# Half of the summed down blocks by seven products, two of the four weight sums by adding transfers

## The chip, the cores and the metric

The kernel runs on one core of one Trainium2 chip. The metric is the device time of one execution in microseconds (us), lower is better; the time of the kernel before is the median of three runs. Engines are named as in the profile: PE is TensorE, ACT is ScalarE, DVE is VectorE, POOL is GpSimd, SP is SyncE, whose queue issues nearly all loads.

## The reference, cut to what matters

```python
x = x + einsum(merged, w_out)                        # three kinds of mixers, 16 heads
x = x + cross_attention(rms_norm(x, g_cross), mem_n, w_cq, w_ckv, w_co)
u = jnp.einsum('bsd,df->bsf', rms_norm(x, g_mlp[l]), w_up[l])
x = x + jnp.einsum('bsf,fd->bsd', jnp.square(jax.nn.relu(u)), w_down[l])
return rms_norm(x, g_final)
```

There is one layer, 256 tokens and a width of 2048; the hidden width of the last block (the MLP) is 8192. All is float32. The MLP's two products take more than half of the time, and the change lies in the second of them, the down product hidden (256 x 8192) by w_down (8192 x 2048), but for one small move ahead of it.

## The kernel before, in words

**Splitting.** Each weight is used as a high part plus a low part. A megabyte of weights is loaded by SP into one of four `staged` slots. ACT writes the high part of a half (128 x 1024) to `w_high`, DVE subtracts it from the staged half and writes `w_low`, and PE multiplies: high by high, low weight by high activation, high weight by low activation. `w_high` and `w_low` hold four halves each; half h uses place h % 4, so ACT may split it only when PE is done with half h - 4. The counts are semaphores: `landed` (a slot has arrived), `high_ready`, `low_ready`, `half_done`. SP waits on `low_ready`, since a slot is free when its last half was split.

**The MLP.** The hidden width is done in four quarters. In a quarter, 16 up jobs (two halves each) make 16 tiles of 128 hidden channels, `part_b`; each goes from PE through ACT and DVE (`up`). Then comes the quarter's share of the down product. Quarter 3 does it plainly, into `x`. Quarters 0 to 2 (`SUMMED_QUARTERS`) do it with tokens as rows: outputs are 128 tokens by 512 columns, one matmul 128 x 512 at a time.

**A group.** In such a quarter there are two groups g of 1024 output columns. A group has four units of 512 hidden channels (four tiles). Three units are done directly by `r_half`: four halves of 12 matmuls each, into the PSUM tensors `extra[0..3]`. One unit, unit 0, is taken as a 2 x 2 block product (two halves of the tokens, of the channels and of the columns) and done by seven products in place of eight (Winograd's form): `s_half`, seven halves of 6 matmuls each. That needs sums of activations (`sums_of_tokens`, into `part_s`) and four sums of weight blocks (`sum_of_weights`, DVE, in place in the staged slots). Halves 0 to 2 multiply plain blocks, halves 3 to 6 are unit 1, halves 7 to 10 multiply the summed blocks (`H_SUMS`), halves 12 to 19 are units 2 and 3 (`H_B`, `H_C`). In all a group has 7 x 6 + 12 x 12 = 186 matmuls. At its end the results go by twelve DVE adds of 128 x 512 (`step`) into `y`, which is `values`. In quarter 3 PE turns `y` back by transposes between the up jobs, and DVE adds it to `x`.

**What sets the order.** It is written out by hand: each engine runs its own list in order, with semaphore waits. In the down part SP loads a unit as two transfers of 1 MB (`load_unit`, of w_down, 2 KB pieces), each as soon as its slot's last half is split. DVE's list is `down_group`: weight sums, low splits and steps, with the splits of the next group (`next_group`) or quarter at its end. PE's list is `down_group` too.

**Ahead of the MLP.** `norm_sum` is one small matmul on PE that sums the squares of the tokens, which POOL accumulates. It stands right after the first job that uses the new x, both before the cross attention (N_X1) and before the MLP (N_X2). POOL also clears `y` (line 411), and DVE waits for that before its first split of the MLP.

## Time and profile before

| | us |
|---|---|
| median of 3 runs | 1203.58 (1203.50 to 1203.62) |
| the profiled execution's own time | 1203.42 |
| its span in the trace | 1201.6 |
| PE busy | 1182.1, 98% of the span |
| DVE busy | 853.1, 71% |
| ACT busy | 628.7, 52% |
| POOL busy | 177.8, 15% |
| DMA, mean rate | 187 GB/s |

The granted TensorE clock was 0.998 of full. The span is 1.8 us less than the time of the same execution. Busy time of an engine in the page is time in which at least one of its instructions runs; successive matmuls overlap, so the mean duration of a matmul in the groups (389 ns) is more than the distance between two of them. That distance is read from the timeline. In the trace the three summed quarters' down parts lie near 571 to 656, 747 to 833 and 922 to 1008 us.

### The profile page before, as it was taken

The numbers are of one execution on the slowest core, as the hardware profiler recorded it, in microseconds if no ns is written. First come the engines' busy times: TensorE is split into PE (matmuls) and PEld (weight loads), VectorE is DVE, ScalarE is ACT, GpSimd is POOL, SyncE is SP. The second block draws the span as 40 slices with busy tenths as digits, with TensorE's granted clock in tenths as the row PEclk, the third lists the DMA queues.
The fourth block names the chain that finished last, engine by engine and source line by source line (L and its number), as shares of the span: only waits on it lengthen the run. The fifth ranks groups of instructions, "written<-read, shape, count | busy, mean of one in ns | idle before, by whom it ended". The sixth has DMA issues, their size and how long they took to land.

```text
span 1201.6 us, 19272 instructions
## 1 busy us (share of the span) xinstructions
PE 1182.1 (98%) x6776; PEld 1035.6 (86%) x6776; DVE 853.1 (71%) x1149; ACT 628.7 (52%) x927; POOL 177.8 (15%) x177
## 2 busy tenths in 40 slices
PE   9999999999999999999999999999999999999996
PEld 7888899999989889888788888788888888888885
DVE  5758766786668867676887666877767787666554
ACT  6445455555645657555544555544655454555442
POOL 2907400030322404200000000000000000000341
PEclk9999999999999999999999999999999999999999
DMA  9674553443644543456456454547543746555531
GB/s 357 252 260 173 196 175 140 162 154 140 246 162 165 181 159 142 151 198 209 166 176 253 175 181 168 210 149 271 175 176 139 264 157 220 191 182 187 198 140 70
DMA packets 51455, 224.43 MB, mean 187 GB/s; under 512 B 3792, under 2 KB 4176, under 8 KB 31696
## 3 DMA queue, kind: packets, MB, share of 16 engines
q1 hardware_dynamic: 50688, 220.22, 50.8%
q10 hardware_dynamic: 720, 3.59, 0.8%
q8 instruction: 30, 0.49, 0.2%
q14 instruction: 17, 0.14, 0.0%
HBM read 221.69 MB, written 2.10 MB: 186 GB/s over the span
## 4 chain that ended last, share of the span: by engine, by line
PE 93%; DVE 3%; ACT 1%; issue 1%; POOL 1%; DMA 1%; SPq 0%; DVEq 0%; ACTq 0%; POOLq 0%
PE bank L1301 16%; PE bank L1298 16%; PE bank L1299 15%; PE extra L1557 6%; PE extra L1559 5%; PE extra L1558 5%; PE bank L1303 4%; PE bank L1305 4%; PE bank L1304 4%; PE bank L1344 3%; PE bank L1346 3%; PE bank L1345 3%; DVE w_low L813 1%; PE bank L1570 1%; PE bank L1571 1%
## 5 line engine op out<-in xcount | busy, mean ns | idle before, releaser
L813 DVE TENSOR_TENSOR w_low<-staged,w_high 128x1024 fp32r<-128x1024 f32 x311 | 390.0, 1269 | 145.5 <-ACT w_high L433 134.9
L433 ACT ACTIVATE w_high<-staged 128x1024 fp32r<-128x1024 f32 x304 | 314.6, 1053 | 189.8 <-PE bank L1301 81.2
L1299 PEld LDWEIGHTS bank<-part_a,w_low 128*128 128x128 f32 x1408 | 264.6, 188 | 61.4
L1298 PE MATMUL bank<-part_a,w_high 128*128 128x512 f32 x704 | 281.0, 399 | 0.0
L1301 PE MATMUL bank<-part_a,w_high 128*128 128x512 f32 x704 | 278.5, 396 | 0.0
L1299 PE MATMUL bank<-part_a,w_low 128*128 128x256 f32 x1408 | 276.8, 278 | 0.0
L719 ACT ACTIVATE w_high<-staged 128x1024 fp32r<-128x1024 f32 x114 | 118.9, 1058 | 108.9 <-PE extra L1559 92.0
L1133 DVE TENSOR_TENSOR w_low<-staged,w_high 128x1024 fp32r<-128x1024 f32 x114 | 137.4, 1221 | 33.8 <-ACT w_high L719 32.6
L361 POOL TENSOR_TENSOR squares<-x 128x256 f32<-128x256 f32 (+1 forms) x31 | 37.3, 1204 | 685.2 <-DVE x L1257 661.3
L1298 PEld LDWEIGHTS bank<-part_a,w_high 128*128 128x128 f32 x704 | 133.7, 190 | 0.6 <-DVE w_low L813 0.3
L1301 PEld LDWEIGHTS bank<-part_a,w_high 128*128 128x128 f32 x704 | 132.0, 187 | 0.0
L1557 PE MATMUL extra<-w_high,part_b 128*128 128x512 f32 x288 | 112.7, 391 | 3.2 <-DVE w_low L1133 2.2
L1559 PE MATMUL extra<-w_high,part_b 128*128 128x512 f32 x288 | 112.1, 389 | 0.0
L1558 PE MATMUL extra<-w_low,part_b 128*128 128x512 f32 x288 | 112.1, 389 | 0.0
L1303 PE MATMUL bank<-part_a,w_high 128*128 128x256 f32 x384 | 110.2, 287 | 0.1
L1305 PE MATMUL bank<-part_a,w_low 128*128 128x256 f32 x384 | 108.7, 283 | 0.0
L1304 PE MATMUL bank<-part_a,w_high 128*128 128x256 f32 x384 | 108.6, 283 | 0.0
L1098 DVE TENSOR_TENSOR part_b<-hidden,part_b 128x256 f32 (+1 forms) x64 | 27.2, 426 | 71.6 <-ACT part_b L701 71.6
L1303 PEld LDWEIGHTS bank<-part_a,w_high 128*128 128x128 f32 x384 | 73.7, 192 | 0.5 <-POOL part_a L375 0.4
L1304 PEld LDWEIGHTS bank<-part_a,w_high 128*128 128x128 f32 x384 | 73.6, 192 | 0.1
L1305 PEld LDWEIGHTS bank<-part_a,w_low 128*128 128x128 f32 x384 | 73.6, 192 | 0.0
L1557 PEld LDWEIGHTS extra<-w_high,part_b 128*128 128x128 f32 x288 | 54.0, 188 | 16.7 <-issue 5.1
(201 smaller groups left out, 1775.1 us busy)
## 6 DMA issues: line engine op xcount, KB each, us to landing
staged<-in_wup SPq DMA_DIRECT2D x64, 1024.0 KB, 4.8
staged<-in_wdown SPq DMA_DIRECT2D x64, 1024.0 KB, 5.0
staged<-in_wqk SPq DMA_DIRECT2D x32, 1024.0 KB, 4.8
staged<-in_wv SPq DMA_DIRECT2D x12, 1024.0 KB, 5.4
staged<-in_wbc SPq DMA_DIRECT2D x8, 1024.0 KB, 4.8
staged<-in_wmk SPq DMA_DIRECT2D x4, 1024.0 KB, 4.7
staged<-in_woa SPq DMA_DIRECT2D x4, 1024.0 KB, 4.8
staged<-in_wcq SPq DMA_DIRECT2D x4, 1024.0 KB, 4.8
```

Of the source, the lines that this page charges most:

```text
L433: nc.scalar.activation(w_high[:, job % 2, cols], staged[:, job % 4, cols], ACT.Copy).then_inc(high_ready, 1)
L813: tt(w_low[:, job % 2, cols], staged[:, job % 4, cols], f32(w_high[:, job % 2, cols]), ALU.subtract).then_inc(low_ready, 1)
L1133: tt(half_4d(w_low, h), src, f32(half_4d(w_high, h)), ALU.subtract).then_inc(low_ready, made)
L1298: mm(out[:, :], high, both, start=first, stop=False)
L1299: last = mm(out[:, 0:T], low, part[:, slot(kt), 0, :], start=False, stop=False)
L1301: last = mm(out[:, :], high, both, start=False, stop=last_tile)
L1303: mm(out[:, 0:T], high, part[:, slot(kt), 0, :], start=first, stop=False)
L1304: mm(out[:, 0:T], high, part[:, slot(kt), 1, :], start=False, stop=False)
L1305: last = mm(out[:, 0:T], low, part[:, slot(kt), 0, :], start=False, stop=last_tile)
L1557: mm(out[:, :], part_b[:, kt, 0, tokens], high, start=opens, stop=False)
L1558: mm(out[:, :], part_b[:, kt, 0, tokens], low, start=False, stop=False)
L1559: last = mm(out[:, :], part_b[:, kt, 1, tokens], high, start=False, stop=ends)
```

## The change

**Units 0 and 2 by seven products.** A group is now two pairs, each of one unit by seven products and one unit done directly: four pairs in a quarter (`PAIRS`), each with halves 0 to 2 plain blocks, 3 and 4 the direct unit's first part, 5 to 8 the summed blocks (`H_T`), 10 and 11 the direct unit's rest. A pair has 7 x 6 + 4 x 12 = 90 matmuls, a group 180. Sums of activations are made for both units.

**Products summed in PSUM.** The seven products of pair 0 stay in their PSUM places and those of pair 1 are added there. DVE then adds all eight places to `y` in four adds of 128 x 1024 a group, and `y` now holds the raw products in eight blocks a group; a second array `y_right` is added for it. The recombination (`combine`, seven DVE operations a group) is done once, during quarter 3. The transposes there follow in its second half.

**Two weight sums by transfers.** The sign form of the sums is changed so that all are additions. Two of the four are made by POOL's queue: `weights_onto` issues transfers from DRAM with an adding write onto the staged block, two of 128 x 4 x 128 float32 (256 KB, in 512 B pieces) for each sum. The first sum waits for the landing of the second slot; the second one waits also for the split of the first block. ACT waits on `right_sum` and `upper_sum`, and DVE on `upper_sum` ahead of its own two sums.

**Slots.** The seven-product unit always uses slots 0 and 1, the direct one slots 2 and 3.

**Smaller moves.** `norm_sum` for N_X1 and N_X2 stands in the middle of the first half of the second job, no longer behind the first job. DVE's wait for the clearing of `y` stands ahead of the down part. At the end of the up jobs, the low split of half 3 (`r_tile`) stands ahead of the last `up` on ACT and DVE. `rope` shares its place with later tensors, and three loops on DVE and ACT are unrolled.

```diff
-GROUP_HALVES = 20
-GROUP_STEPS = 12
+PAIRS = 4
+PAIR_HALVES = 12
+GROUP_STEPS = 4
+H_B11, H_B21, H_B22, H_R, H_T, H_R_END = 0, 1, 2, 3, 5, 10
+SLOT_S, SLOT_R = 0, 2
...
+            def load_down(q):
+                for k in range(PAIRS):
+                    load_unit(q, k, k % 2 * 2, SLOT_S, (-2, -2) if k else (-6, -4))
+                    load_unit(q, k, k % 2 * 2 + 1, SLOT_R, (H_T - PAIR_HALVES, 0) if k else (-2, 0))
...
+            def weights_onto(q, k, to, n, row, signal):
+                unit = k % 2 * 2
+                src = wdown_in[bass.ds(q * 16 + (k // 2 * 8 + 4 * n), 4), :,
+                               512 * unit:512 * (unit + 1)].rearrange("o p (a b c) -> p b a o c", a=2, b=2)
+                for pair in range(2):
+                    pool.dma_start(to[:, pair, :, :], src[:, row, pair, :, :], accum_op=ALU.add).then_inc(signal, 16)
+
+            with pool.Fori(0, SUMMED_QUARTERS) as q:
+                for k in range(PAIRS):
+                    pool.wait_ge(landed[SLOT_S + 1], q * 128 + 16 * (JOB_MLP // 4 + 4 + k + 1))
+                    weights_onto(q, k, by_pair(SLOT_S + 1, 0), 1, 1, right_sum)
+                    pool.wait_ge(low_ready, down_half(q, k) + 1)
+                    weights_onto(q, k, by_pair(SLOT_S, 0), 1, 0, upper_sum)
...
+                    if n < 2:
+                        act.wait_ge((upper_sum, right_sum)[n], q * 128 + 32 * (k + 1))
+                    else:
+                        act.wait_ge(weight_made, q * 8 + (2 * k + n - 1))
+                    down_high(q, k, H_T + n, by_pair(SLOT_S + col, row), 2 if n == 3 else 1)
...
+            def down_pair(q, k, ahead):
+                last = k % 2
+                r_tile(q, k, 1)
+                sum_of_weights(q, k, 2)
+                s_sum(q, k, 0)
+                sum_of_weights(q, k, 3)
+                for n in range(1, 4):
+                    s_sum(q, k, n)
+                r_tile(q, k, 2)
+                if last:
+                    step(q, k, 0)
+                r_tile(q, k, 3)
+                if last:
+                    step(q, k, 1)
                 ahead(0)
+                if last:
+                    step(q, k, 2)
                 ahead(1)
...
                 ahead(2)
+                if last:
+                    step(q, k, 3)
                 ahead(3)
...
+                if opens:
+                    pe.wait_ge(y_step, steps)
+                pe.wait_ge(s_low, q * 4 + (unit + 2))
+                s_half(q, k, H_B22, extra[2], sum_of(unit, 3), opens)
...
-                if s == 0:
-                    norm_sum(N_X1, extra[3])
```

In `load_unit` the numbers in brackets are counted from the pair's own first half: -2 is met when the last summed block (half 8, which counts twice) of the pair before is split.

POOL, between the clearing of `y` and the loop over the last norm. Before, nothing stands there:

```order
L411 MEMSET values 128x4096 [waits cross_o]
L354 MEMSET acc 128x256 [waits sum_ready]
L413 UNCONDITIONAL_BRANCH [waits acc_clear]
```

Now, the last of the four pairs in the loop over the quarters (each pair has these rows):

```order
L432 ISA [waits landed1]
L432 DMA staged<-in_wdown 128x4x128
L432 ISA
L432 DMA staged<-in_wdown 128x4x128
L438 REGISTER_ALU
L432 ISA [waits low_ready]
L432 DMA staged<-in_wdown 128x4x128
L432 ISA
L432 DMA staged<-in_wdown 128x4x128
```

Four issues a pair have come to POOL's queue, 48 in all. `landed1` is the semaphore of the second slot.

DVE, from the last tile of the up jobs into the first group of a quarter. Before:

```order
521 L1091 TENSOR_TENSOR spare<-spare,bank3 128x256 [waits up_moved]
522 L1094 SCALAR_TENSOR_TENSOR spare<-spare,factor 128x256 [waits up_added]
523 L1098 TENSOR_TENSOR part_b<-hidden,part_b 128x256 [waits hid_high]
524 L1148 TENSOR_TENSOR staged<-staged 128x2x4x128
525 L1132 REGISTER_ALU
526 L1133 TENSOR_TENSOR w_low<-staged,w_high 128x1024 [waits high_ready]
527 L1148 TENSOR_TENSOR staged<-staged 128x2x4x128
528 L1132 REGISTER_ALU
529 L1133 TENSOR_TENSOR w_low<-staged,w_high 128x1024 [waits high_ready]
530 L1148 TENSOR_TENSOR staged<-staged 128x2x4x128 [waits weight_made]
```

Now, at the same place:

```order
547 L1157 TENSOR_TENSOR w_low<-staged,w_high 128x1024 [waits high_ready]
548 L1114 REGISTER_ALU
549 L1115 TENSOR_TENSOR spare<-spare,banks 128x256 [waits up_moved]
550 L1118 SCALAR_TENSOR_TENSOR spare<-spare,factor 128x256 [waits up_added]
551 L1122 TENSOR_TENSOR part_b<-hidden,part_b 128x256 [waits hid_high]
552 L1156 REGISTER_ALU [waits y_clear]
553 L1157 TENSOR_TENSOR w_low<-staged,w_high 128x1024 [waits high_ready]
554 L1167 ISA
555 L1171 TENSOR_TENSOR staged<-staged 128x2x4x128 [waits upper_sum]
556 L1156 REGISTER_ALU
557 L1157 TENSOR_TENSOR w_low<-staged,w_high 128x1024 [waits high_ready]
```

The split of half 3 (row 526 before, 547 now) has moved ahead of the last tile's three operations, and the first weight sum that DVE makes waits for POOL's transfers; the splits of the summed blocks are queued behind it.

## Rows read from the trace of the kernel before

**Rows 1.** The page: busy time of the engines, and the chain that ended last.
```profile
PE 1182.1 (98%) x6776; PEld 1035.6 (86%) x6776; DVE 853.1 (71%) x1149; ACT 628.7 (52%) x927; POOL 177.8 (15%) x177
...
PE 93%; DVE 3%; ACT 1%; issue 1%; POOL 1%; DMA 1%; SPq 0%; DVEq 0%; ACTq 0%; POOLq 0%
```

**Rows 2.** Busy time by stretch: an up part, a down part.
```profile
core 0: us, PE busy (x) PEld busy (x) DVE busy (x) ACT busy (x) POOL busy (x), PEclk, DMA share, GB/s
660.00:747.00 87.00, 87.00 (x501) 75.90 (x501) 58.74 (x87) 49.12 (x78) 0.00 (x0) 1.00 0.51 181
747.00:834.00 87.00, 85.91 (x381) 70.55 (x380) 70.29 (x73) 42.43 (x44) 0.00 (x0) 1.00 0.56 202
```

**Rows 3.** Timeline of PE: a down part's start, group 1's start, next quarter.
```profile
747.36 0.39 PE L1570 MATMUL bank<-w_high,part_b 128*128 128x512 f32 x1
...
751.22 0.39 PE L1572 MATMUL extra<-w_high,part_s 128*128 128x512 f32 x1
752.70 0.49 PE L1557 MATMUL extra<-w_high,part_b 128*128 128x512 f32 x1 [1.09 <-DVE w_low L1133]
...
790.96 0.39 PE L1570 MATMUL bank<-w_high,part_b 128*128 128x512 f32 x1
...
833.24 0.39 PE L1298 MATMUL bank<-part_a,w_high 128*128 128x512 f32 x1
```

**Rows 4.** Timeline of PE, ACT and DVE: one half's end, and the next split.
```profile
766.20 0.39 PE L1572 MATMUL bank<-w_high,part_s 128*128 128x512 f32 x1
...
766.62 1.06 ACT L719 ACTIVATE w_high<-staged 128x1024 fp32r<-128x1024 f32 x1 [1.60 <-PE bank L1572]
...
767.72 2.59 DVE L1133 TENSOR_TENSOR w_low<-staged,w_high 128x1024 fp32r<-128x1024 f32 x2 [1.36 <-ACT w_high L719]
```

**Rows 5.** Timeline of DVE at 750 us: sums and splits back to back.
```profile
750.21 1.22 DVE L1148 TENSOR_TENSOR staged<-staged 128x1024 f32<-128x1024 f32 x1
751.35 1.22 DVE L1133 TENSOR_TENSOR w_low<-staged,w_high 128x1024 fp32r<-128x1024 f32 x1
752.48 1.22 DVE L1148 TENSOR_TENSOR staged<-staged 128x1024 f32<-128x1024 f32 x1
```

**Rows 6.** w_down's loads, 744 to 792 us: issues on SP, and time to landing.
```profile
766.52 0.93 SPq L317 DMA_DIRECT2D staged<-in_wdown  x2
770.48 0.37 SPq L317 DMA_DIRECT2D staged<-in_wdown  x1
...
DMA to landing us min/median/max: 5.0/5.1/7.8
```

**Rows 7.** The same stretch by windows of 2 us (columns as in rows 2).
```profile
770.00:772.00 2.00, 2.00 (x11) 1.63 (x10) 1.97 (x4) 1.36 (x2) 0.00 (x0) 1.00 1.05 403
772.00:774.00 2.00, 2.00 (x11) 1.65 (x10) 1.97 (x3) 1.06 (x1) 0.00 (x0) 1.00 1.08 382
```

**Rows 8.** DMA issues by size: median us from issue to landing.
```profile
out<-values SPq DMA_DIRECT2D x3, 512.0 KB, 2.8
...
out<-values SPq DMA_DIRECT2D x1, 256.0 KB, 2.1
```

**Rows 9.** Timeline of PE at the two norm sums.
```profile
407.64 0.40 PE L1301 MATMUL bank<-part_a,w_high 128*128 128x512 f32 x1
408.91 0.70 PE L1353 MATMUL extra<-acc,square 128*128 128x256 f32 x2 [0.88 <-POOL acc L370]
...
486.41 0.40 PE L1301 MATMUL bank<-part_a,w_high 128*128 128x512 f32 x1
487.94 0.70 PE L1353 MATMUL extra<-acc,square 128*128 128x256 f32 x2 [1.13 <-POOL acc L370]
```

**Rows 10.** Timeline of DVE, then PE, behind the second norm sum.
```profile
491.77 1.23 DVE L813 TENSOR_TENSOR w_low<-staged,w_high 128x1024 fp32r<-128x1024 f32 x1 [5.28 <-POOL values L411]
...
496.62 0.40 PE L1301 MATMUL bank<-part_a,w_high 128*128 128x512 f32 x1
497.03 0.50 PE L1298 MATMUL bank<-part_a,w_high 128*128 128x512 f32 x1
```

**Rows 11.** Groups of instructions: a step of before on DVE.
```profile
L1176 DVE TENSOR_TENSOR values<-values,extra 128x512 f32<-128x512 f32 x24 | 16.5, 686 | 3.3 <-PE extra L1559 2.9
```

More of the change, by code:

```diff
@@ L307, in _, with load_up @@
             stream(wco_in, JOB_CO, CROSS)
-            def load_up(q):
-                with sp.Fori(0, QUARTER // 4) as i:
+            def load_up(q, first):
+                if first:
+                    for s in range(4):
+                        load(wup_in[q * 16 + s, :, :], mlp(q), JOB_MLP + s)
+                else:
+                    for s, free in enumerate((-2, -2, H_T - PAIR_HALVES, 0)):
+                        sp.wait_ge(low_ready, mlp(q)(2) + (H_MLP + free))
+                        sp.dma_start(staged[:, s, :], wup_in[q * 16 + s, :, :]).then_inc(landed[s], 16)
+                with sp.Fori(1, QUARTER // 4) as i:
@@ L1306, in half_job, with job_of @@
                 return last
-            def job_of(off, job, n_out, part, ready=None, wide=True, slot=lambda kt: kt):
+            def job_of(off, job, n_out, part, ready=None, wide=True, slot=lambda kt: kt, between=None):
                 pe.wait_ge(taken, off(1) + (n_out + 1))
@@ L1317, in job_of @@
                     half_job(off, job, half, bank[job % 4], part, 8 * half, wide=wide,
-                             slot=slot, waits=waits).then_inc(half_done, 1)
+                             slot=slot, waits=waits, between=None if half else between).then_inc(half_done, 1)
             def short_jobs(job, n_out, part, at, waits={}):
@@ L1516, in _ @@
                     job_of(none, JOB_CQ + s, OUT_CQ + s, part_a,
[L1517 removed]
+                           x1_low if s == 0 else None, slot=slot_x1, between=N_X1 if s == 1 else None)
                 else:
```

447 lines of the change are left out of this document (210 added, 237 removed).

## The prediction

> **What bounds the kernel now.** I read the page first: PE is busy for 98% of the span and is 93% of the chain that ended last [rows 1]. Then the stretches: in an up part PE never rests, in a down part it rests 1.1 us, and DVE, the next busiest, works 70.3 of 87 us there [rows 2]. So a matmul less is worth its full distance as long as DVE, ACT and the loads keep up, and the down part has the least room for that. The distance between two matmuls is what counts, not the 389 ns of one: group 1 of quarter 1 runs from 790.96 to 833.24 us, 42.28 us for 186 matmuls, 0.2273 us each [rows 3].
>
> **Part 1, fewer matmuls.** 6 fewer in each of 6 groups: 36 x 0.2273 = 8.2 us less on PE.
>
> **Part 2, half 3 split earlier.** At the start of a down part PE has issued its last matmul of half 2 at 751.22 and could go on at 751.45, but starts half 3 at 752.70 [rows 3]. It waits for a DVE split queued behind the last tile's operations. These change places, so 1.25 us goes in each of three quarters, 3.8 us.
>
> **Part 3, the norm sums.** PE could go on at 407.87 and 486.64 but waits for POOL until 408.91 and 487.94, 1.04 and 1.30 us [rows 9]. In the middle of the next half-job POOL is done. Behind the second sum there is no slack: PE waits a little again at 497.03 for a DVE split (it could have gone on at 496.85), and DVE had itself started at 491.77 only, when POOL's clearing of `y` was over [rows 10]. The norm sum itself comes no earlier than now, but that wait for the clearing goes from there. I keep 1.1 of the 1.30: 2.1 us in both (bounds 1.2 and 2.3).
>
> **Part 4, DVE and ACT.** A step of 128 x 512 takes 686 ns [rows 11], twelve in a group; now four adds of 1024 columns take some 1.2 us each, as a split does [rows 5]. DVE's list for a group was 19 splits, 4 sums and 12 steps, 23 x 1.135 + 12 x 0.70 = 34.5 us (1.135 us is the distance of two operations back to back [rows 5]). Now it is 22 splits, 4 sums and 4 steps, 30 x 1.135 = 34.1 of 40.9 us. In quarter 3 the recombination adds 14 operations, some 11 us, over eight up jobs of 5.4 us in which DVE is busy two thirds of the time [rows 2]; I cost it at nothing, with DVE's rest as cover (without it, up to 11 us). The second unit's sums of activations lie there too, in each quarter. The longer clearing of `y` is needed only at the first down part.
>
> If nothing else were late, the sum would be 8.2 + 3.8 + 2.1 = 14.1 us less.
>
> **Part 5, where the loads now stand.** This decides. I follow one pair on PE from its start: halves 0 to 2 end at 4.09, halves 3 and 4 at 9.55, the summed halves 5 to 8 at 15.0, the pair at 20.46. Between a half's end on PE (766.43) and the next split there are 0.2 us to ACT, 1.1 to DVE's start and 1.2 for DVE [rows 4, 5], 2.5 in all. Half 8 may be split when half 4 is done, so its split is over at 9.55 + 2.5 = 12.1. That frees slots 0 and 1, and only then SP issues the next pair's two loads and the one for slot 2 behind them. A load lands 5.1 us after its issue, the second of two issued together after 7.8 [rows 6], a further one 2.7 later (1.05 MB at the 390 GB/s of [rows 7]). So slot 0 lands at 17.2, slot 1 at 19.9, slot 2 at 22.6. Half 3 of the next pair is then ready at 22.6 + 1.1 + 1.2 + 0.1 = 25.0 and due at 20.46 + 4.09 = 24.55: half a microsecond late with no adding transfer in the way. And behind an odd pair DVE has nine operations queued from 13.6 on (splits 10, 11, 0, 1, 2 and the four steps), until 23.8; PE waits for the last step ahead of half 2, due at 23.2.
>
> **Part 6, the adding transfers.** They start when slot 1 has landed. DVE's first sum waits for them, with the splits of halves 5 to 8 queued behind it: sum, split, sum, split, split, split, 6 x 1.135 + 0.1 = 6.9 us. The last of these is what frees the slots for the next pair. So there is a loop: split of half 8, loads (7.8), transfers (X), DVE (6.9). Its length is c = 14.7 + X a pair, against 20.46 on PE. X is the time from slot 1's landing to the landing of all four adding transfers (256 KB each). A quarter's down part has three such loops, 12.1 us ahead of them and 6.9 behind (half 8 and halves 10, 11 on PE): 19.0 + 3c, against 85.88 now (747.36 to 833.24 [rows 3]). Over three quarters, with part 3: 9c - 200.7 - 2.1, which is 9X - 70.5. It breaks even at X = 7.8. Ahead of pair 0 the loads come during the up jobs, and its transfers are hidden. The two ACT waits are off the path, as ACT's splits run ahead of DVE's.
>
> No transfer of POOL's queue and no adding one is in this trace, so X is bounded. From below: four issues 0.47 us apart (SP's: 0.93 for two [rows 6]) and a plain 256 KB transfer, 2.1 us [rows 8], 3.5 us. From above: four times the moving time for each, behind SP's loads, 16.1 us. A plain 256 KB costs 0.7 us of moving (2.8 less 2.1 for 256 KB more) and 1.4 around it [rows 8]. An add reads the block in DRAM and the staged block, so I take 1.4 us each, 5.6 for four. SP's two loads for slots 2 and 3 stand ahead of them on the same engines, 5.4 us of which 2.4 have passed when slot 1's landing is seen (5.1 less 2.7): 3.0. The end costs 1.4 and POOL's first issue 0.5. X = 3.0 + 5.6 + 1.4 + 0.5 = 10.5 us, c = 25.2, and the change is 9 x 10.5 - 70.5 = +24 us. The value is nearer to the lower bound since its row is a transfer of this size; the upper one is a guess at how much a piece of 512 B and an add can cost.
>
> On the same price the Trainium skill has a rule: in "DMA: Bandwidth & Descriptors", section "Anatomy of one DMA — SWDGE (gpsimd) path", a transfer issued by GpSimd takes about 2.0 us plus its bytes at 436 GB/s, an estimate of 2.6 us here. With four of them overlapping at the issue distance above, X would be 4.1 us and the loop would not bind, which is the first rival. Against it, "Collectives: The Full Stack", section "Why ReduceScatter is half of AllGather", says that an adding transfer is slower because it needs two source reads. No run here shows either yet.
>
> **The rivals.**
>
> (a) The transfers fit, X under 7.8. Then the late slot 2 and the steps of part 5 stay: 0.5 to 1.1 us for each of nine pairs and 0.6 to 0.9 for three odd pairs, 6.3 to 12.6 us, off 14.1. That gives 2 to 8 us less, and I take 5: 1198 us. For it: the plain 256 KB transfer of 2.1 us. Against it: SP's loads fill the engines (a DMA share of 1.05 and 1.08 [rows 7]) just when the transfers start.
>
> (b) All of the gain comes, 14.1 us: 1189.3 us. That needs loads some 1 us quicker than the landing times of rows 6.
>
> (c) The transfers are far slower than their plain price, X over 16. The mechanism is the same loop, at the wait of DVE's first sum in each of nine pairs; it passes 1280 us at X = 16.3, and X = 25 gives 9 x 25 - 70.5 = +154, 1358 us. Then pair 0's transfers show too. For it: pieces of 512 B, where w_down's loads have 2 KB.
>
> **How the numbers follow.** The profiled execution took 1203.42 us, 0.16 below the median of the runs, so the sum can be set against either. Forecast: 1203.4 + 24 = 1227.5 us. Chances: X between 8 and 16, slower by 2 to 77 us, 0.62; near break-even 0.04; (a) 0.15; (b) 0.06; (c) 0.13. A measurement of this kernel can tell about 0.2%, 2.4 us, from no change. Part of (a) lies within that: faster 0.18, same 0.07, slower 0.75. The range goes from 1197 to 1280: it leaves out (b), the quick end of (a), and (c). The forecast's own range is 1206 to 1280.
>
> **What would show it.** In the profile of the changed kernel: 1080 matmuls of 128 x 512 in the summed quarters, distance unchanged; no wait at half 3 of the first pair of a quarter; PE waiting at half 5, the first summed block, in pairs 1 to 3 for a DVE split, DVE's sum in turn for a transfer, together some 4 to 5 us a pair; pairs 25 us apart, slot loads issued right behind half 8's split. Wrong if the transfers land within 7.8 us of slot 1 (then half 3 and half 2 have the waits), if the longest wait stands at another half, or if the up part of quarter 3 becomes longer by more than 1 us (part 4).

## The result, and the profile after

The changed kernel took 1251.53 us (median of 4 runs, 1250.67 to 1252.63), the kernel before, run beside it, 1203.54 (1203.20 to 1203.62). The ratio is 1.0398, 95% interval 1.0383 to 1.0413: 48.0 us slower. The forecast was slower, 1227.5 us, with a range of 1197 to 1280. So the direction and the mechanism held, and half of the size was missing.

The page of the changed kernel, busy time and the chain that ended last, to be read against [rows 1]:

```profile
PE 1196.0 (96%) x6740; PEld 1037.2 (83%) x6740; DVE 869.1 (70%) x1155; ACT 644.4 (52%) x945; POOL 244.0 (20%) x226
...
PE 72%; DMA 12%; issue 6%; DVE 5%; ACT 3%; POOL 1%; SPq 0%; POOLq 0%; DVEq 0%; ACTq 0%
```

The 36 matmuls are gone (6776 before, 6740 now), and yet PE is busy for longer, because part of its work now runs at a lower clock (below). In the chain PE fell from 93% to 72%, and DMA rose from 1% to 12%. Two groups of the page name it, first an instruction group, then the DMA issues with KB each and median us to landing:

```profile
L432 POOL DMA_DIRECT2D staged<-in_wdown x48 | 62.6, 1879 | 478.9 <-DMA staged<-in_wdown 455.7
...
staged<-in_wdown SPq DMA_DIRECT2D x64, 1024.0 KB, 5.6
...
staged<-in_wdown POOLq DMA_DIRECT2D x48, 256.0 KB, 6.9
```

PE's waits of the changed kernel (engine, line and releaser; us in total, times, longest):

```profile
PE banks L1597 <- DVE w_low L1157: 30.2, 12, 4.2
PE extras L1584 <- DVE w_low L1157: 4.3, 5, 1.1
PE extras L1597 <- DVE values L1186: 1.7, 3, 0.7
```

L1597 multiplies the blocks of the seven products, plain and summed, and L1584 the direct unit. The three down parts show the whole loss (columns as in [rows 2]):

```profile
570.31:673.52 103.21, 89.51 (x361) 69.60 (x359) 66.83 (x61) 45.08 (x47) 15.59 (x12) 0.95 0.70 187
762.81:865.30 102.49, 89.95 (x362) 70.93 (x360) 66.76 (x61) 44.91 (x47) 15.63 (x12) 0.93 0.69 186
954.58:1055.63 101.05, 88.92 (x361) 69.47 (x360) 67.50 (x61) 45.59 (x47) 15.95 (x13) 0.95 0.68 186
```

They are 306.75 us together, where before they were 257.6 (85.8 and twice 85.9; the second is 747.36 to 833.24 in [rows 3]): 49.2 us more. The first down part starts 2.1 us earlier than before, and the stretch from the end of the last down part to the end of the span is as long as it was (193.4 us). DVE is busy for 67 us of these 102, so the amount of its work is no bound, as the sum of part 4 said. PE's idle time is 38.4 us of the 306.8; its 360 matmuls a quarter, 81.8 us at 0.2273 us each, keep it busy for 89.5 in the mean. Most of that excess goes with the lower granted clock (0.93 to 0.95): e10 below, at 1.00, has 83.5.

The loop that the forecast rested on stands in the timelines. First DVE's first sum in each pair of a quarter (some of the expectations call a pair a super-unit), with what its idle time ended on (start us, us, engine line op out<-in xcount):

```profile
576.65 1.22 DVE L1171 TENSOR_TENSOR staged<-staged 128x1024 f32<-128x1024 f32 x1
...
603.50 1.23 DVE L1171 TENSOR_TENSOR staged<-staged 128x1024 f32<-128x1024 f32 x1 [5.96 <-DMA staged<-in_wdown]
...
630.11 1.22 DVE L1171 TENSOR_TENSOR staged<-staged 128x1024 f32<-128x1024 f32 x1 [5.33 <-DMA staged<-in_wdown]
...
657.54 1.23 DVE L1171 TENSOR_TENSOR staged<-staged 128x1024 f32<-128x1024 f32 x1 [6.45 <-DMA staged<-in_wdown]
```

The pairs follow each other at 26.85, 26.61 and 27.43 us, against the 20.46 that PE needs. One turn of the loop, from the chain of waits between 610 and 637 us:

```profile
610.46 0.37 SPq L328
...
610.87 7.41 DMA staged<-in_wdown
...
618.94 0.06 POOL staged L432
...
621.17 8.91 DMA staged<-in_wdown
...
635.82 1.23 DVE w_low L1157
637.06 0.37 SPq L328
```

SP issues when half 8 is split, the second of the two loads has landed 7.8 us later, from 618.3 POOL issues and the transfers move until 630.1, and DVE's sums and splits take 6.95 us until SP is released again. That is 7.8 + 11.8 + 7.0 = 26.6.

### The profile page after: what moved, and what is told of

Its sections match the earlier page's. It is cut to its first block, busy times and chain, and to the rows that moved or that the text cites. A ratio compares the mean times of both kernels' runs of the same rounds, so it can differ in the third digit from the quotient of the medians.

```text
span 1249.0 us, 19107 instructions
## 1 busy us (share of the span) xinstructions
PE 1196.0 (96%) x6740; PEld 1037.2 (83%) x6740; DVE 869.1 (70%) x1155; ACT 644.4 (52%) x945; POOL 244.0 (20%) x226
## 3 DMA queue, kind: packets, MB, share of 16 engines
q0 software_dynamic: 25344, 12.59, 8.1%
## 4 chain that ended last, share of the span: by engine, by line
PE 72%; DMA 12%; issue 6%; DVE 5%; ACT 3%; POOL 1%; SPq 0%; POOLq 0%; DVEq 0%; ACTq 0%
PE banks L1326 15%; PE banks L1329 15%; PE banks L1327 15%; DMA staged<-in_wdown 10%; PE banks L1331 5%; PE banks L1333 5%; PE banks L1332 5%; PE banks L1372 3%; PE banks L1374 3%; PE banks L1373 3%; DVE w_low L1157 2%; ACT w_high L748 1%; POOL staged L432 1%; DMA staged<-in_wup 1%; DVE staged L1171 1%
## 5 line engine op out<-in xcount | busy, mean ns | idle before, releaser
L837 DVE TENSOR_TENSOR w_low<-staged,w_high 128x1024 fp32r<-128x1024 f32 x311 | 390.1, 1269 | 135.5 <-ACT w_high L461 130.6
L1327 PEld LDWEIGHTS banks<-part_a,w_low 128*128 128x128 f32 x1408 | 264.6, 188 | 61.7
L1326 PE MATMUL banks<-part_a,w_high 128*128 128x512 f32 x704 | 280.5, 398 | 1.4 <-DVE w_low L837 1.4
L1329 PE MATMUL banks<-part_a,w_high 128*128 128x512 f32 x704 | 278.5, 396 | 0.0
L1327 PE MATMUL banks<-part_a,w_low 128*128 128x256 f32 x1408 | 276.8, 278 | 0.0
L1157 DVE TENSOR_TENSOR w_low<-staged,w_high 128x1024 fp32r<-128x1024 f32 x132 | 157.4, 1221 | 50.3 <-ACT w_high L748 49.8
L432 POOL DMA_DIRECT2D staged<-in_wdown x48 | 62.6, 1879 | 478.9 <-DMA staged<-in_wdown 455.7
L1326 PEld LDWEIGHTS banks<-part_a,w_high 128*128 128x128 f32 x704 | 133.7, 190 | 2.7 <-DVE w_low L837 2.5
L1329 PEld LDWEIGHTS banks<-part_a,w_high 128*128 128x128 f32 x704 | 131.9, 187 | 0.0
L1331 PE MATMUL banks<-part_a,w_high 128*128 128x256 f32 x384 | 110.1, 287 | 0.1
L1333 PE MATMUL banks<-part_a,w_low 128*128 128x256 f32 x384 | 108.7, 283 | 0.0
L1332 PE MATMUL banks<-part_a,w_high 128*128 128x256 f32 x384 | 108.6, 283 | 0.0
L1584 PE MATMUL extras<-w_high,part_b 128*128 128x512 f32 x192 | 75.5, 393 | 4.3 <-DVE w_low L1157 4.3
L1585 PE MATMUL extras<-w_low,part_b 128*128 128x512 f32 x192 | 74.8, 390 | 0.0
L1586 PE MATMUL extras<-w_high,part_b 128*128 128x512 f32 x192 | 74.8, 389 | 0.0
L1331 PEld LDWEIGHTS banks<-part_a,w_high 128*128 128x128 f32 x384 | 73.7, 192 | 0.5 <-POOL part_a L387 0.4
L1332 PEld LDWEIGHTS banks<-part_a,w_high 128*128 128x128 f32 x384 | 73.6, 192 | 0.1
L1333 PEld LDWEIGHTS banks<-part_a,w_low 128*128 128x128 f32 x384 | 73.6, 192 | 0.0
L725 ACT ACTIVATE hidden<-spare 128x256 f32<-128x256 f32 x64 | 26.8, 418 | 85.6 <-DVE spare L1118 85.6
```

The source lines that it names most:

```text
L432: pool.dma_start(to[:, pair, :, :], src[:, row, pair, :, :], accum_op=ALU.add).then_inc(signal, 16)
L837: tt(w_low[:, job % 2, cols], staged[:, job % 4, cols], f32(w_high[:, job % 2, cols]), ALU.subtract).then_inc(low_ready, 1)
L1157: tt(half_4d(w_low, h), src, f32(half_4d(w_high, h)), ALU.subtract).then_inc(low_ready, made)
L1326: mm(out[:, :], high, both, start=first, stop=False)
L1327: last = mm(out[:, 0:T], low, part[:, slot(kt), 0, :], start=False, stop=False)
L1329: last = mm(out[:, :], high, both, start=False, stop=last_tile)
```

## The experiments

All are compared with the kernel before, run on the same chip beside them. Times are medians.

| run | us | ratio to before, interval |
|---|---|---|
| changed kernel | 1251.53 | 1.0398 (1.0383 to 1.0413) |
| e1_plain | 1227.41 | 1.0197 (1.0180 to 1.0214) |
| e2_slot2_first | 1255.97 | 1.0430 (1.0413 to 1.0448) |
| e3_dve_sums | 1227.81 | 1.0192 (1.0175 to 1.0209) |
| e4_small_moves | 1201.86 | 0.9985 (0.9976 to 0.9995) |
| e5_upper_first | 1231.15 | 1.0231 (1.0214 to 1.0248) |
| e6_right_by_dve | 1222.06 | 1.0154 (1.0137 to 1.0170) |
| e7_rotated | 1239.11 | 1.0294 (1.0277 to 1.0311) |
| e8_rotated_upper_first | 1225.14 | 1.0183 (1.0166 to 1.0200) |
| e9_before_four_first | 1197.02 | 0.9946 (0.9932 to 0.9959) |
| e10_rotated_right_by_dve | 1201.56 | 0.9984 (0.9974 to 0.9994) |
| e11_rotated_dve_sums | 1203.64 | 1.0001 (0.9992 to 1.0011) |

### e1: the same transfers without the adding

```diff
-                    pool.dma_start(to[:, pair, :, :], src[:, row, pair, :, :], accum_op=ALU.add).then_inc(signal, 16)
+                    pool.dma_start(to[:, pair, :, :], src[:, row, pair, :, :]).then_inc(signal, 16)
```

> The changed kernel with the adding write left out of POOL's 48 transfers: they overwrite the staged block (so two of the four weight sums are not made), all waits and sizes as they are. Theory: the loop of a pair (DVE's split of half 8, slot loads, transfers X, DVE) sets the time, and X = 11.8 us is 0.6 to POOL's start, 5.2 of four issues of 1.30 us, and 6.0 to the last landing. If the add itself (two reads) makes the 6.0 long, a plain write ends X near 0.6 + 5.2 + 2.1 = 7.9 us: nine loops by 3.9 us, 35 us less, 1216 us. Rival 1, queueing behind SP's two loads makes it long: X falls by the second read alone, at most 0.7 us each for the last two, 1.4: 1239 us. Rival 2, the small pieces (512 B) and not the add: no change, 1251 us.

Measured: 1227.41 us, 24 us less than the changed kernel, midway between the 1216 of the theory and the 1239 of the first rival. POOL's issues of one pair, from the timeline of POOL, first in the changed kernel and then in e1:

```profile
591.89 5.18 POOL L432 DMA_DIRECT2D staged<-in_wdown  x4 [23.50 <-DMA staged<-in_wdown]
```

```profile
591.72 2.96 POOL L432 DMA_DIRECT2D staged<-in_wdown  x4 [24.61 <-DMA staged<-in_wdown]
```

And DVE's first sums in e1:

```profile
601.11 1.22 DVE L1171 TENSOR_TENSOR staged<-staged 128x1024 f32<-128x1024 f32 x1 [3.75 <-DMA staged<-in_wdown]
...
624.78 1.22 DVE L1171 TENSOR_TENSOR staged<-staged 128x1024 f32<-128x1024 f32 x1 [2.46 <-DMA staged<-in_wdown]
```

Windows of e1 behind the loads (columns as in [rows 2]):

```profile
596.00:598.00 2.00, 1.73 (x8) 1.42 (x9) 1.35 (x2) 0.00 (x0) 0.00 (x0) 1.00 1.04 303
598.00:600.00 2.00, 2.00 (x10) 1.69 (x9) 0.00 (x0) 0.00 (x0) 0.00 (x0) 1.00 0.60 168
```

An issue takes 0.74 us in place of 1.30, and this loop is 23.7 us in place of 26.6; in the mean of all nine it is 24.3 in place of 26.8, so X is 9.6 us where the adding form needs 12.1. The plain transfers move at 303 GB/s from 596 to 598 us and are nearly through by 600, the adding ones at 166 to 192 until 602 (the windows are shown further below). So the adding form costs 2.5 us for four transfers, nine times, and half of the whole loss. What in it costs that, the adding itself or its smaller packets, is not shown: the plain transfers went in 80 packets each, the adding ones in 528. Nor does e1 show what makes the other half; e3, below, loses as much without any transfer of POOL's, though with two more sums a pair on DVE.

### e2 and e5: other orders of the same transfers

e2 has SP load slot 2 of the next pair as soon as half 4 is split, ahead of slots 0 and 1:

```diff
                 for k in range(PAIRS):
+                    if k:
+                        load_unit(q, k, k % 2 * 2 + 1, SLOT_R, (H_T - PAIR_HALVES, 0), (0,))
                     load_unit(q, k, k % 2 * 2, SLOT_S, (-2, -2) if k else (-6, -4))
-                    load_unit(q, k, k % 2 * 2 + 1, SLOT_R, (H_T - PAIR_HALVES, 0) if k else (-2, 0))
+                    load_unit(q, k, k % 2 * 2 + 1, SLOT_R, (H_T - PAIR_HALVES, 0) if k else (-2, 0),
+                              (1,) if k else (0, 1))
```

> The changed kernel with SP's load of slot 2 for pairs 1 to 3 issued ahead of the loads of slots 0 and 1 (its slot is free much earlier, after the split of half 4 of the pair before), so that 1 MB less stands ahead of the adding transfers on the DMA engines; SP's loop over the quarters is unrolled for it. Theory that the transfers queue behind SP's loads: X falls by up to 2.7 us, nine loops, 24 us less, 1227 us, and PE's wait at half 3 of pairs 1 and 3 goes. Rival, X is POOL's issues and the transfer itself: X stays at 11.8, the time at 1250 us, only the wait moves from half 3 to half 5.

Measured: 1255.97 us, 4.4 slower than the changed kernel, where I had expected 1227 and the rival said 1250. Windows of e2 after POOL's issues at 592.06 (columns as in [rows 2]), then DVE's first sum:

```profile
594.00:596.00 2.00, 2.00 (x11) 1.69 (x10) 2.00 (x2) 0.51 (x1) 2.00 (x3) 1.00 1.25 161
596.00:598.00 2.00, 2.00 (x11) 1.65 (x10) 0.14 (x1) 0.00 (x0) 1.24 (x1) 1.00 1.31 156
...
600.00:602.00 2.00, 1.09 (x5) 0.56 (x3) 0.00 (x0) 0.00 (x0) 0.00 (x0) 1.00 1.09 305
```

```profile
606.22 1.23 DVE L1174 TENSOR_TENSOR staged<-staged 128x1024 f32<-128x1024 f32 x1 [10.08 <-DMA staged<-in_wdown]
```

With fewer loads ahead of them the adding transfers move early (161 and 156 GB/s from 594), but then the load for slot 2 of the next pair, issued at 596.16, comes among them, and the sum can only start at 606.22, 14.2 us after POOL's first issue. The megabyte was moved from ahead of the transfers into them, and nothing was won.

e5 issues the upper sum's transfers ahead of the right one's:

```diff
-                    pool.wait_ge(landed[SLOT_S + 1], q * 128 + 16 * (JOB_MLP // 4 + 4 + k + 1))
-                    weights_onto(q, k, by_pair(SLOT_S + 1, 0), 1, 1, right_sum)
                     pool.wait_ge(low_ready, down_half(q, k) + 1)
                     weights_onto(q, k, by_pair(SLOT_S, 0), 1, 0, upper_sum)
+                    pool.wait_ge(landed[SLOT_S + 1], q * 128 + 16 * (JOB_MLP // 4 + 4 + k + 1))
+                    weights_onto(q, k, by_pair(SLOT_S + 1, 0), 1, 1, right_sum)
```

> The changed kernel with POOL's two sums in the other order: the upper one, which DVE's first sum and half 5 need, is issued first, the right one, needed by half 6, behind it. Waits and sizes as they are. Theory: the transfers run after SP's loads at 1.4 us each, the upper sum then lands 2.8 us earlier; the right one, landing where the upper one did, holds half 6 by some 0.5 us; each of nine loops is 2.3 us shorter: 21 us less, 1231 us. Rival, half 8's split needs all four transfers in any order: nothing changes, 1251 us.

Measured: 1231.15 us, as expected. DVE's sum waits for the upper sum alone, so only two of the four transfers stand in the loop ahead of it: it starts at 600.64 in place of 603.50, and what comes late of the other two is a wait of 0.5 us for the right sum's half behind it. The order of two pairs of issues on POOL is worth 20 us here.

### e3 and e6: sums by DVE in place of transfers

e3 has all four sums made by DVE and no transfer by POOL; e6 only the right one.

```diff
             def down_pair(q, k, ahead):
...
+                sum_of_weights(q, k, 0)
                 r_tile(q, k, 1)
-                sum_of_weights(q, k, 2)
+                sum_of_weights(q, k, 1)
                 s_sum(q, k, 0)
-                sum_of_weights(q, k, 3)
-                for n in range(1, 4):
-                    s_sum(q, k, n)
+                sum_of_weights(q, k, 2)
+                s_sum(q, k, 1)
+                sum_of_weights(q, k, 3)
+                s_sum(q, k, 2)
+                s_sum(q, k, 3)
```

> The changed kernel with all four weight sums of a pair made by DVE, none by transfers; POOL issues nothing. Theory: the loop loses X and gets two DVE operations. From slot 1's landing at 7.8 us DVE has the split of half 2, then, from slot 2's landing at 10.5, ten operations of 1.135 us to the end of half 8's split: c = 10.5 + 1.1 + 11.4 = 23 us, one more with steps between: 9 x 23.5 - 202.7 = +9 against before, 1205 to 1222 us. Rival, the loads or the lower granted clock make the down part long and not X: less than 10 us are gained, 1240 us or more.

```diff
             def down_pair(q, k, ahead):
                 last = k % 2
+                tt(by_pair(SLOT_S + 1, 0), by_pair(SLOT_S + 1, 0), by_pair(SLOT_S + 1, 1),
+                   ALU.add).then_inc(right_sum, 1)
                 r_tile(q, k, 1)
...
-                    weights_onto(q, k, by_pair(SLOT_S + 1, 0), 1, 1, right_sum)
```

> The changed kernel with the right sum made by DVE (one operation ahead of half 4's split, while it would wait anyway) and the upper one alone by two transfers. Theory: X loses two transfers of 1.4 us each and two issues, about 3.4 us; the DVE operation is hidden in DVE's wait for the upper sum: nine loops, 31 us less, 1221 us. Rival, it is DVE that has no room (four sums on DVE gave 1227.8 us): the operation costs its 1.1 us in each of 12 pairs: 1233 us.

Measured: e3 1227.81 us, above the 1205 to 1222 that I had expected, e6 1222.06, as expected. At e3 I took PE's many waits of 0.5 to 1.1 us for a VectorE at its limit. Its timeline says otherwise:

```profile
591.35 2.36 DVE L1141 TENSOR_TENSOR w_low<-staged,w_high 128x1024 fp32r<-128x1024 f32 x2 [3.65 <-ACT w_high L735]
...
638.57 2.36 DVE L1141 TENSOR_TENSOR w_low<-staged,w_high 128x1024 fp32r<-128x1024 f32 x2 [3.70 <-ACT w_high L735]
```

DVE stands still for 3.7 us, for ACT, and ACT for a load; the two rows are two pairs apart, and in the pair between, which has the four steps on DVE, it is 1.8 us. The loop of the slots' reuse (split of half 8, then the load of both slots of the seven-product unit, then the splits) is there without any transfer of POOL's; it is only shorter (23.7 us from the first sum at 597.91 to the next pair's at 621.63). That gave e7.

### e7 and e8: rotated slots

The seven-product unit has two loads, called its first and second S block here. The first S block of the next pair goes into the slot that half 4's split frees, no longer into one that the sums hold until half 8's:

```diff
-SLOT_S, SLOT_R = 0, 2
+SLOTS_OF = ((0, 1, 2, 3), (2, 0, 1, 3), (1, 2, 0, 3), (0, 1, 2, 3))
...
                 for k in range(PAIRS):
+                    s_slots, r_slots = SLOTS_OF[k][:2], SLOTS_OF[k][2:]
+                    if k:
+                        load_unit(q, k, k % 2 * 2, s_slots, (H_T - PAIR_HALVES, -2), (0,))
+                        load_unit(q, k, k % 2 * 2, s_slots, (H_T - PAIR_HALVES, -2), (1,))
+                    else:
+                        load_unit(q, k, 0, s_slots, (-6, -4))
+                    load_unit(q, k, k % 2 * 2 + 1, r_slots, (-2, 0))
```

> The changed kernel with slots that rotate from pair to pair, (0,1,2,3), (2,0,1,3), (1,2,0,3), (0,1,2,3) for the summed unit's two and the direct unit's two: the next pair's first block goes to the slot that is free after half 4's split, and only the second one and the direct unit's first wait for half 8's split. POOL's order as in the change, SP's loop over the quarters unrolled. Theory: the loop that sets the time is slot release, load, transfers, DVE; with the first block loaded some 7 us earlier the loads ahead of the transfers are fewer, and slot 1's landing comes 2.7 us earlier. The upper sum would land near 29.4 us in the pair's clock and is due at 27.5: 1.9 us late in nine pairs: 1194 + 17 = 1211 us (1200 to 1225). Rival, the engines' total work (four loads and four transfers in the same place) sets the landing, as in the run with slot 2's load moved: 1245 us or more.

e8 is e7 with the order of e5 on POOL.

> The same rotated slots with the upper sum's transfers first. They wait for the split of the first block, over at 17.7 us of the pair before, and land near 25 where 27.5 is due, so the waits at half 5 go; the right sum is at most 0.5 us late for half 6. Theory: all that is left of the change's cost is the step behind odd pairs: 14.1 us less than before but for some 4 to 6 us, 1194 to 1199 us, faster than the kernel before. Rival, POOL's own issues (1.30 us each, and 3.9 us of standing still once a quarter) hold pairs whatever the slots: 1205 to 1215 us.

Measured: 1239.11 and 1225.14 us, both far above what I had expected (1211, and 1194 to 1199); the first stays under its rival's 1245, the second is above its rival's 1205 to 1215 too. The windows of e7 behind POOL's first issue at 590.19:

```profile
592.00:594.00 2.00, 2.00 (x11) 1.65 (x10) 0.52 (x1) 1.61 (x2) 2.00 (x3) 1.00 1.05 387
594.00:596.00 2.00, 2.00 (x11) 1.65 (x10) 1.84 (x2) 0.51 (x1) 1.37 (x2) 1.00 1.30 188
596.00:598.00 2.00, 2.00 (x10) 1.66 (x9) 0.00 (x0) 0.00 (x0) 0.00 (x0) 1.00 1.46 185
...
600.00:602.00 2.00, 1.57 (x7) 0.95 (x6) 0.00 (x0) 0.00 (x0) 0.00 (x0) 1.00 1.12 341
```

and DVE's next sum there:

```profile
605.31 1.23 DVE L1176 TENSOR_TENSOR staged<-staged 128x1024 f32<-128x1024 f32 x1 [9.46 <-DMA staged<-in_wdown]
```

Two things show. The loads still come first (387 GB/s until 594), the adding transfers then fill the engines for six microseconds at 185 to 200 GB/s, and a further load comes before the last of them has ended: 15.1 us from POOL's first issue to the sum. And the loop is not gone. The second S block still waits for half 8's split, and the right sum is added onto just that block, so every pair still has a split, a load and an adding transfer in a row, with one load in it in place of two. Its second turn is 605.31 to 629.40, 24.1 us. In e8 the upper sum is out of that row, but the right one is not, and ACT waits for it (4.3 us ahead of its split at 603.19).

### e10 and e11: the rotation with the right sum, or all sums, by DVE

e10 is e7 with the edit of e6, e11 is e7 with the edit of e3.

> The changed kernel with the loads into rotated slots of e7, and the second weight sum by VectorE instead of POOL's adding transfers, as in e6: what is left to the adding transfers is 512 KB a super-unit, two issues of POOL. Theory (DMA order): e7 and e8 lost most of what the rotation should give because POOL's adding transfers moved only behind SP's loads that were already in the queues (first pair of e7: share 1.05 at 387 GB/s till 594, then 1.3 to 1.46 at 185 to 200 GB/s for 6 us, so 15.1 us from POOL's first issue at 590.19 to VectorE's sum at 605.31). With half as many transfers that queue costs 2.9 us less and PE's waits of 4 to 6 us at the first pair fall to 1 to 3; VectorE, with 4.9 us more of sums a quarter, keeps its waits of 0.5 to 1.1 us at some eight places a quarter, as in e6. Down parts 89 to 92 us, time 1211 to 1219, say 1215. Rival 1 (VectorE is the bound of the hybrid): the same as e6, 1220 to 1224, waits of PE all for w_low with VectorE without idle time ahead of them. Rival 2: both were independent losses and go together, down parts of 86 to 87 us and 1200 to 1205, which would bring the family level with the kernel before.

> The changed kernel with all four weight sums by VectorE, as in e3, and the rotated slots of e7: POOL adds nothing, no transfer reads a block a second time. Theory: in e3 the bound was not VectorE's work but the loop of a slot's reuse: VectorE stood 3.65 to 3.70 us before half splits at 591.35 and 638.57, for ACT, which stood 3.8 us for the load of a block whose slot the sums had held. Its work in two super-units of e3 is 21.7 and 17.7 us (597.91 to 645.4 without its idle time), 19.7 in the mean against the 20.5 us that PE needs for one. With the load early, that wait is gone, and what is left are PE's waits of 0.5 to 1 us where VectorE runs through its 21.7 us stretch. Down parts of 84 to 89 us instead of 94.3, 95.8 and 93.6: 1227.8 - 3 x 8 = 1203, range 1196 to 1210. So the adding transfers of e10 (1201.6) would be worth about nothing, 2.3 us of VectorE a super-unit against waits for DRAM. Rival 1 (VectorE is the bound): the waits stay as in e3 at every fourth half and the time is 1215 to 1228. Rival 2 (transfers were the whole rest): below 1196, level with the kernel of e9.

Measured: e10 1201.56 us, in the second rival's 1200 to 1205 and 13 us below what I had expected; e11 1203.64, as expected. PE's waits in the down parts, of e10, then of e11:

```profile
PE banks L1602 <- DVE w_low L1160: 3.9, 6, 1.6
PE extras L1602 <- DVE values L1189: 1.8, 3, 0.6
```

```profile
PE banks L1587 <- DVE w_low L1146: 2.9, 6, 0.6
...
PE extras L1587 <- DVE values L1173: 1.3, 3, 0.5
```

The 30.2 us of waits of the changed kernel for the low parts of these blocks are down to 3 or 4. So it was the place of the loads and transfers that cost the time, and not the seven products for two units: with the right sum on DVE, no transfer has to wait for the late block any more. The down parts are 86.3, 87.9 and 83.7 us in e10 and 86.8, 87.1 and 85.8 in e11, against 85.8 and twice 85.9 before. All that 2.7 us less of matmuls a quarter brings, 8.2 us in all, is spent again where PE waits for DVE: the matmuls that start later than 0.2273 us behind the one before, nearly all of them at the start of a half that a DVE result released, add up to 12.2 us in e10's three down parts and 13.4 in e11's, against 4.2 before. DVE is 29 us (e10) and 42 us (e11) busier than before (882.1 and 894.8 against 853.1 in [rows 1], the recombination of quarter 3 among it).

Two adding transfers a pair, in place of one sum by DVE, gain 2.1 us here (e10 against e11, whose intervals of the ratio just touch) and 5.8 us with the old slots (e6 against e3). And e10 and e11 have the small moves in them. The kernel before with an order of the same kind, e9 below, takes 1197.02 us, 4.5 less than e10: no run of this study shows the new arithmetic ahead of the old one.

### e4 and e9: the small moves, in the kernel before

e4 is the kernel before with the three smaller moves: `norm_sum` in the middle of the next job, DVE's wait for the clearing later, and half 3's split ahead of the last `up`.

```diff
                 for n in range(count):
+                    if between is not None and n == count // 2:
+                        norm_sum(between, extra[3])
...
-                if s == 0:
-                    norm_sum(N_X1, extra[3])
...
+                    if s == 3:
+                        r_tile(q, 0, 3, SLOT_RA[0], 0)
                     up(q, 3, s)
...
                         sum_of_weights(q, 0, 0)
-                        r_tile(q, 0, 3, SLOT_RA[0], 0)
...
+                dve.wait_ge(y_clear, 1)
                 down_group(q, 0, next_group(q))
```

> The kernel before with the change's small moves alone: the two norm sums in the middle of the next half-job, DVE's wait for the clearing of y ahead of the down part, and the split of half 3 ahead of the last tile's operations on ACT and DVE. One unit of four by seven products, all as before. Theory (parts 2 and 3 of the prediction): 3.8 + 2.1 = 5.9 us less, 1197.7 us (0.995 of before). Rival, the wait at half 3 comes back at the first weight sum, which is now behind: 2.1 us less, 1201.4 us.

Measured: 1201.86 us, the rival's value. Timeline of DVE, then of PE, at the start of the first down part:

```profile
574.89 2.35 DVE L1148 TENSOR_TENSOR staged<-staged 128x1024 f32<-128x1024 f32 x2
577.16 1.22 DVE L1133 TENSOR_TENSOR w_low<-staged,w_high 128x1024 fp32r<-128x1024 f32 x1
...
578.43 0.50 PE L1558 MATMUL extra<-w_high,part_b 128*128 128x512 f32 x1 [1.15 <-DVE w_low L1133]
```

The wait at half 3 is gone and stands at half 4, as long as before: two of DVE's differences of weights are ahead of its split. In the changed kernel no sum of DVE's stands there, so there the move gained what it should.

e9 puts half 4's split ahead of the first difference too:

```diff
                     else:
+                        r_tile(q, 0, 3, SLOT_RA[0], 1)
                         sum_of_weights(q, 0, 0)
...
-                sum_of_weights(q, g, 1)
-                r_tile(q, g, 3, ra, 1)
-                sum_of_weights(q, g, 2)
-                r_tile(q, g, 3, ra, 2)
-                sum_of_weights(q, g, 3)
-                r_tile(q, g, 3, ra, 3)
+                if g:
...
+                else:
+                    r_tile(q, g, 3, ra, 2)
+                    sum_of_weights(q, g, 1)
+                    r_tile(q, g, 3, ra, 3)
+                    sum_of_weights(q, g, 2)
+                    sum_of_weights(q, g, 3)
```

> The kernel before with the small moves of e4 (norm sums behind the first half of the next job, the wait for the cleared outputs later, half 3's split ahead of the last up chunk's) and one more: for the first super-unit of a quarter the split of half 4 stands ahead of VectorE's first difference of weight blocks, those of halves 5 and 6 each behind one difference. Theory: what swallowed the gain of half 3's move in e4 was a wait of PE for half 4's split (1.24 us on PE at 578.43, 753.62 and 928.83), which came late because two differences (2.36 us) stood ahead of it on VectorE. Half 4's high part is ready by 575.4, its split then ends near 576.6, and PE reaches the half at 577.1; the half of difference later still leaves the sums' splits (due from 585.3) more than 1 us. So the wait goes in all three pairs: 1201.9 - 3 x 1.25 = 1198.1, first down at 570.3 as before the change of order, the down part 84.7 to 84.9 long instead of 86.0. Rival: the wait moves on once more, to half 5 or 6 or to the first weight sum, and the time stays at 1201 to 1202. A second rival: only the first quarter gains, since later ones start with VectorE behind, 1200.5.

Measured: 1197.02 us, as expected (1198.1), 6.5 us below the kernel before (ratio 0.9946, 0.9932 to 0.9959) and the fastest of this study. DVE's timeline:

```profile
575.86 1.23 DVE L1133 TENSOR_TENSOR w_low<-staged,w_high 128x1024 fp32r<-128x1024 f32 x1 [0.52 <-ACT w_high L719]
577.00 1.22 DVE L1148 TENSOR_TENSOR staged<-staged 128x1024 f32<-128x1024 f32 x1
```

PE no longer waits anywhere in the three down parts, which last 84.5 us each. What beat the kernel before is an order of a few instructions, with none of the new arithmetic.

## Why the prediction was right, and where it fell short

**Part 1 held.** PE runs 36 matmuls fewer, 0.227 us apart where its clock is full (for instance from 668.64 to 672.50, 17 steps of 0.2271). The saving is real, and covered by waits.

**Part 2 held in the changed kernel,** where no wait stands at half 3 of a quarter's first pair. That it would be worth 3.8 us by itself did not: e4 shows the same wait at the next half, until e9 moved that too.

**Part 3 held.** The first down part starts at 570.31 us, where it was 572.39: 2.08 us, predicted 2.1.

**Part 4 held.** Quarter 3 and what follows take 193.4 us as before, with the 14 recombinations in it, and the steps cost no more than said.

**Part 5 held in its order and was short in its head.** Slot 2 is late as said: the five waits at L1584 (up to 1.1 us) are its waits, and the three for `values` (up to 0.7 us) are those for the last step ahead of half 2. But half 8's split of the first pair ends 13.2 us after the pair's start and not at 12.1. The sum let it hang on PE's half 4 alone. In the trace DVE starts its list at 575.50, late because of the last tile's operations, and then runs without a rest until 583.5, so the length of DVE's list decides:

```profile
575.50 1.23 DVE L1157 TENSOR_TENSOR w_low<-staged,w_high 128x1024 fp32r<-128x1024 f32 x1 [0.53 <-ACT w_high L748]
...
580.05 3.49 DVE L1157 TENSOR_TENSOR w_low<-staged,w_high 128x1024 fp32r<-128x1024 f32 x3
```

The first sum stands 6.34 us into the down part, forecast 5.2: 1.1 us in each quarter, 3.4 in all.

**Part 6: the mechanism was right, X was mis-sized.** The load (7.8 us) and DVE's share (6.9, measured 6.95) are as forecast. X was taken as 10.5, and over the nine loops it comes to 12.1 (26.8 - 14.7; the nine take 241.1 us). This is the term that failed, and the windows between POOL's first issue at 591.9 and the sum at 603.5 say which part of it:

```profile
592.00:594.00 2.00, 2.00 (x11) 1.58 (x10) 1.33 (x2) 0.44 (x1) 2.00 (x3) 1.00 1.05 386
594.00:596.00 2.00, 1.50 (x7) 0.91 (x5) 0.82 (x1) 1.92 (x2) 2.00 (x3) 1.00 1.05 381
596.00:598.00 2.00, 1.54 (x7) 1.28 (x8) 1.54 (x2) 0.09 (x1) 1.07 (x1) 1.00 1.44 192
598.00:600.00 2.00, 2.00 (x11) 1.65 (x10) 0.00 (x0) 0.00 (x0) 0.00 (x0) 1.00 1.44 177
600.00:602.00 2.00, 2.00 (x10) 1.50 (x8) 0.00 (x0) 0.00 (x0) 0.00 (x0) 1.00 1.34 166
```

Until 596 the engines carry only SP's loads at their full rate, then for some 5.7 us the adding transfers, 1 MB at 166 to 192 GB/s. That is 1.4 us each, the price that was taken. The 3.0 us for the loads ahead of them was too little: two megabytes stood behind slot 1, and they were through at about 596, 4.7 us after slot 1's landing near 591.3. The sum had counted 2.4 us of their 5.4 as past when that landing is seen; it was about 0.7. Once a quarter there is more: POOL stands still for 3.9 us between two issues, and that loop is 1.2 us longer (27.4 to 27.8 us, against 25.9 to 26.9 for the other six). Timeline of POOL:

```profile
645.43 3.91 POOL L432 DMA_DIRECT2D staged<-in_wdown  x3 [21.31 <-DMA staged<-in_wdown]
653.22 1.30 POOL L432 DMA_DIRECT2D staged<-in_wdown  x1 [3.88 <-issue]
```

In all the loops cost 14.3 us more than forecast (241.1 against 9 x 25.2). A rule of the Trainium skill ("DMA: Bandwidth & Descriptors", section "Anatomy of one DMA — SWDGE (gpsimd) path") had stood as a rival here: by it a transfer would take an estimated 2.6 us. The traces have a median of 5.9 us to landing for the plain ones of e1 and 6.9 for the adding ones, both with SP's loads ahead of them in the same engines, so neither shows what one takes alone. The Trainium skill also says ("Collectives: The Full Stack", section "Why ReduceScatter is half of AllGather") that a ReduceScatter is the slower one because its add needs two source reads. That would fit 2.5 us more for four of them, but no run here shows reads, and e1 changed the packets too.

**The tail was short too.** Behind the last first sum I had 6.9 us of DVE and 6.9 of PE, 13.8; measured were 16.0, 15.6 and 15.0, 5.2 us more in all. Windows of 657 to 669 us show what was missing:

```profile
657.00:661.00 4.00, 1.01 (x4) 0.83 (x5) 3.46 (x4) 2.95 (x3) 0.00 (x0) 0.95 0.01 1
661.00:665.00 4.00, 4.00 (x13) 2.87 (x12) 3.47 (x4) 1.32 (x2) 0.00 (x0) 0.63 0.00 0
665.00:669.00 4.00, 4.00 (x19) 3.31 (x18) 3.17 (x3) 1.86 (x2) 0.00 (x0) 1.00 0.79 283
```

After PE had stood still for 4.2 us, the clock granted was 0.63 of full in the mean from 661 to 665, a mixture of its two levels of 1.2 and 2.4 GHz: 13 matmuls in four microseconds where full clock has 17 or 18. Inside the loops that costs nothing, as PE waits again at the next pair's half 5, but at the end of a quarter it lies on the path. (This is also why the waits at half 5 are 3.3 us a pair in the mean and not the 4 to 5 that were forecast, although the loop is longer: part of its 6.3 us over PE's 20.46 went into slower matmuls and into the waits at half 3.) The rest is a wait for the first split of the next up job, 0.64 us in quarter 0.

Together 3.4 + 14.3 + 5.2 = 22.9 of the 24.0 us by which the forecast was short of the measured 48.0. Of the 1.1 us that is left, 0.9 is the distance of the traced execution (1250.67 us) from the median (1251.53).

**The rivals.** (a) and (b), in which the transfers fit, fell at once: X is 12.1, and over 7.8 even without the adding (9.6 in e1). (c) did not occur. No rival saw that the loop of the slots loses time without any transfer in it, which e3 shows with 1227.8 us.

## What to carry to other kernels

When a step is added between a load and the operation that frees the slot for the next load, write the loop as a sum (load, step, work until the slot is free) and compare it with the bottleneck engine's period; every microsecond over that counts once a turn, here 6.3 us nine times. Then first change what stands in the loop (another slot, the late block's sum by an engine that has time), before the price of the step itself. And where one wait was taken away at a busy engine's list, look at the next item of that list: in the kernel before the wait only moved by one half until that half's split was moved too.

## What the runs showed of the hardware

- An adding transfer of 256 KB in pieces of 512 B took POOL 1.30 us to issue, a plain one 0.74. The page counts 25344 packets for the 48 adding ones, 528 each, and 3840 for the plain ones, 80 each.
- Adding transfers alone in the queues read w_down at 166 to 192 GB/s with a DMA share of 1.34 to 1.44; SP's loads in the same place go at 381 to 396 GB/s with a share of 1.05. They share the engines with the loads in either order: behind them in the changed kernel (11.6 us from POOL's first issue to the sum), mixed with one in e2 (14.2 us), both in e7 (15.1 us).
- POOL stood still for 3.8 to 3.9 us ahead of the 16th, the 32nd and the 44th adding issue of the changed kernel (653.22, 845.31 and 1010.22 us), with nothing in the trace that it waited for; in e2 at the same places for 2.2 to 2.3 us, in e10, with 24 issues in all, once, for 5.5 us. In e1, whose transfers add nothing, it did so once, for 5.1 us, so it does not need the adding. What it is stays open.
- The granted clock fell behind PE's standstills of 4 us, to means of 0.63 in four microseconds, and was 0.93 to 0.95 in the mean over the changed kernel's down parts, where it had been 1.00 before [rows 2].
